# Attention without gate products: transposes in two places, two raw query buffers, the softmax scale on the queries, the maximum written negated

## The reference

```python
def softmax_probs(q, k, scale):
    s = jnp.einsum('bqhd,bkhd->bhqk', q, k).astype(jnp.float32) * scale
    return jax.nn.softmax(s, axis=-1)
# latent attention: 4 heads of 64 + 32, scale (64 + 32) ** -0.5
p = softmax_probs(qb, k, scale).astype(v.dtype)
return jnp.einsum('bhqk,bkhd->bqhd', p, v)
# differential attention: 4 heads with 2 maps of width 32, scale 32 ** -0.5
p = softmax_probs(q1b, k1, scale) - lam * softmax_probs(q2b, k2, scale)
return jnp.einsum('bhqk,bkhd->bqhd', p.astype(v.dtype), v)
```

## Time and profile before

| | |
|---|---|
| median of three runs | 4644.32 us |
| profiled execution | 4637.01 us, its span 4635.2 us |
| PE busy | 3676.0 us (79%) |
| DVE busy | 1965.0 us (42%) |
| ACT busy | 1243.7 us (27%) |
| POOL busy | 1066.2 us (23%) |
| mean granted clock of TensorE | 0.891 |

### The profile page before, as it was taken

One profiled execution on the slowest core, in us unless ns is written; L12 is line 12 of the kernel. 1 busy time (PEld: TensorE's weight loads), 2 busy tenths in 40 slices (PEclk: granted clock), 3 DMA queues, 4 the chain that ended last, 5 costly groups with the idle time before them and its releaser, 6 DMA issues. The chain is left out here.

```text
span 4635.2 us, 63721 instructions
## 1 busy us (share of the span) xinstructions
PE 3676.0 (79%) x25724; PEld 2856.5 (62%) x25724; DVE 1965.0 (42%) x3281; ACT 1243.7 (27%) x2126; POOL 1066.2 (23%) x1114
## 2 busy tenths in 40 slices
PE   5987987466886999897776878987666879998677
PEld 2764656355675777786662665665455757776565
DVE  4224432455345555203553324432554355554255
ACT  2102321344122323213301202321443223232340
POOL 2001001322113343223401101102331034333250
PEclk7978988688898999998987889998788989999898
DMA  4101013100101111335634101014011121111472
GB/s 165 40 34 42 18 34 94 40 26 18 58 29 59 50 44 45 100 118 164 233 105 159 52 32 45 26 33 116 27 31 37 38 65 50 53 53 52 159 252 91
DMA packets 202584, 334.45 MB, mean 72 GB/s; under 512 B 22976, under 2 KB 96448, under 8 KB 200640
## 3 DMA queue, kind: packets, MB, share of 16 engines
q1 hardware_dynamic: 173504, 283.34, 19.3%
q10 hardware_dynamic: 28800, 47.20, 2.8%
HBM read 249.45 MB, written 81.00 MB: 71 GB/s over the span
## 5 line engine op out<-in xcount | busy, mean ns | idle before, releaser
L89 PE MATMUL ps<-hh,wh_ds 128*128 128x512 f32 (+1 forms) x1600 | 689.3, 431 | 79.9 <-POOL wl_ds L202 28.7
L90 PE MATMUL ps<-hl,wh_ds 128*128 128x512 f32 (+1 forms) x1600 | 617.3, 386 | 0.0
L91 PE MATMUL ps<-hh,wl_ds 128*128 128x512 f32 (+1 forms) x1600 | 616.2, 385 | 0.0
L89 PEld LDWEIGHTS ps<-hh,wh_ds 128*128 128x128 f32 x1600 | 322.0, 201 | 161.3 <-issue 54.7
L90 PEld LDWEIGHTS ps<-hl,wh_ds 128*128 128x128 f32 x1600 | 322.3, 201 | 58.5 <-issue 16.7
L91 PEld LDWEIGHTS ps<-hh,wl_ds 128*128 128x128 f32 x1600 | 319.6, 200 | 58.5
L1060 DVE TENSOR_REDUCE mx_d<-ps 128x1 f32<-128x1280 f32 (+1 forms) x144 | 197.2, 1369 | 252.6 <-PE ps L979 252.5
L200 POOL CAST wh_ds<-raw_ds 128x512 fp32r<-128x512 f32 x160 | 107.8, 674 | 792.4 <-DMA raw_ds<-in_d_wmerge 309.2
L933 PE MATMUL ps<-const,qk_da 128*128 128x128 f32 x656 | 131.3, 323 | 163.3 <-ACT pt_da L1101 161.1
L2009 DVE TENSOR_TENSOR T_dr<-T_dr,ps 64x256 f32<-64x256 f32 x400 | 167.6, 419 | 200.3 <-PE ps L1765 191.0
L1131 ACT ACTIVATE qk_da<-ps,nmx_d 128x1280 f32<-128x1280 f32 (+1 forms) x144 | 177.4, 1232 | 229.2 <-DVE nmx_d L1062 229.1
(11 more groups left out here) (322 smaller groups left out, 7977.1 us busy)
## 6 DMA issues: line engine op xcount, KB each, us to landing
gate_sums<-out_ds ACTq DMA_DIRECT2D x160, 256.0 KB, 2.0
raw_ds<-in_d_wmerge SPq DMA_DIRECT2D x128, 256.0 KB, 2.7
logit_mg<-gate_sums SPq DMA_DIRECT2D x128, 256.0 KB, 3.4
w_mod<-in_d_wmod SPq DMA_DIRECT2D x12, 2048.0 KB, 19.7
R_dr<-decay_rows SPq DMA_DIRECT2D x80, 256.0 KB, 4.4
qk_da<-turned_qk SPq DMA_DIRECT2D x32, 320.0 KB, 7.1
q_raw_da<-turned_qk SPq DMA_DIRECT2D x288, 32.0 KB, 1.8
acc_ou<-merged SPq DMA_DIRECT2D x18, 512.0 KB, 5.2
```

The source lines that it names most:

```text
L89: pe.matmul(out, w_hi, x_hi, start=first, stop=False)
L90: pe.matmul(out, w_hi, x_lo, start=False, stop=False)
L91: return pe.matmul(out, w_lo, x_hi, start=False, stop=last)
```

## The change

- The attentions have no gate products: no plan, loads, cuts, moves, `spot` or `settled`. `Dense.ready` gets another lower limit for a stage that plans nothing.
- Groups of transposes are (0,4), (4,2), (6,4) blocks instead of (0,4), (4,4), (8,2). The middle one goes to the upper half of bank 7, where one map's spread inverses also lie; it waits for the move of the group before it there, and in a tile's first head for the last tile's output. The other two share bank 6.
- PE: with two maps each turn group comes after the last piece of scores of a map, the third at the head's end; with one map after the second and the third piece. Value products of a pair come one in head 0 and one in head 2.
- Differential queries have two raw buffers with a semaphore each and two query slots instead of three.
- The scale is multiplied into the queries: on POOL where latent queries are staged, and by two ACT instructions in `prepare_maps`, before the queries are stored.
- `reduce_max(..., negate=True)` writes the negated maximum; L1062 goes. The first map's sum is written where it is kept, so the copy L1049 goes.
- ACT moves the second and third group between the two exponentials; with one map DVE moves groups 0 and 2 ahead of its maximum and inverts there.

```diff
@@ Dense
-        limit = min(self.upto(point), max(self.start, self.end - 2 * KD))
+        low = self.start if self.end > self.start else 0
+        limit = min(self.upto(point), max(low, self.end - 2 * KD))
@@ attention
-    groups = [(at, min(4, key_tiles - at)) for at in range(0, key_tiles, 4)]
+    groups = [(0, 4), (4, 2), (6, 4)] if key_tiles == NT else [(0, CT)]
-    fill.plan((n_tiles - 1) * SPOTS, KD // SPOTS, (7,))
+    SL = 2 // maps
+    value_at = pieces[-1][0] if maps == 2 or len(pieces) == 1 else pieces[-2][0]
-            def turn_bank(count):
-                return m.ps[:, 6, 0:count * P]
+            def turn_bank(g, count):
+                return m.ps[:, 7, BR:BR + count * P] if g == 1 else m.ps[:, 6, 0:count * P]
@@ SP
-                        if g >= 1:
-                            sp.wait_ge(staged, 2 * g)
+                        if g >= 2:
+                            sp.wait_ge(staged, 2 * (g - 1))
-                            sp.dma_start(q_raw[ROPE * a:ROPE * a + ROPE], src).then_inc(q_in, 16)
-                    fill.load(sp, SPOTS * (i - 1))
+                            sp.dma_start(q_raw[ROPE * a:ROPE * a + ROPE, g % 2], src).then_inc(q_in[g % 2], 16)
@@ PE, main loop
+                        pe.wait_ge(staged, maps * (u + 1))
+                        g = 0
                         for a in range(maps):
+                            if u >= SL:
+                                pe.wait_ge(exp_done, (u - SL) * maps + (a + 1))
+                            for at, width in pieces:
+                                mm = pe.matmul(...)
+                                if at + width == keys:
                                     mm.then_inc(scored, 1)
+                                if a == 0 and i and h % 2 == 0 and at == value_at:
+                                    value(i - 1, h // 2)
+                                if before and g < G and (at + width == keys or maps == 1 and at >= value_at):
+                                    turn(*before, g)
+                                    g += 1
+                        while before and g < G:
+                            turn(*before, g)
+                            g += 1
@@ DVE
-                    dve.reduce_max(mx[:, h, a:a + 1], scores(h, a), AX.X).then_inc(dve_step, 1)
-                    dve.wait_ge(dve_step, n + 1)
-                    dve.tensor_scalar(nmx[:, h, a:a + 1], mx[:, h, a:a + 1], -scale, None, ALU.mult).then_inc(maximum, 1)
+                    dve.reduce_max(nmx[:, h, a:a + 1], scores(h, a), AX.X, negate=True).then_inc(maximum, 1)
...
                         if before:
-                            move(*before, on_dve[:1])
+                            move(*before, on_dve)
+                            if maps == 1:
+                                invert(before[1])
@@ ACT
-                        if i and h == LAG:
-                            fill.move(act, SPOTS * i)
...
                             if before and a == 1:
-                                move(*before, on_act[1:2])
+                                move(*before, on_act[1:])
...
-                        if before and maps == 2:
-                            move(*before, on_act[2:])
@@ prepare_maps
-            sp.wait_ge(rotated, 4)
+            sp.wait_ge(q_scaled, 2)
             sp.dma_start(m.d_qk[:, 0:2], raw[0]).then_inc(q_out, 16)
@@ ACT
+            for j in range(2):
+                act.wait_ge(rotated, 2 * (j + 1))
+                act.activation(qk[:, j], qk[:, j], ACT.Copy, scale=ROPE ** -0.5).then_inc(q_scaled, 1)
```

More of the change, by code:

```diff
@@ L834, in attention @@
     on_dve = [g for g in range(G) if g not in on_act]
+    SL = 2 // maps
+    value_at = pieces[-1][0] if maps == 2 or len(pieces) == 1 else pieces[-2][0]
     LAG = 2
     PAIRS = HEADS // 2
-    UNITS = HEADS * maps
-    SPOTS = 4
-    fill = m.dense
-    fill.plan((n_tiles - 1) * SPOTS, KD // SPOTS, (7,))
     with ExitStack() as st:
         sb = lambda n, s, d=F32: st.enter_context(nc.sbuf_tensor(f"{n}_{name}{l}_{t0}", s, d))
-        mx = sb("mx", [P, HEADS, maps])
         nmx = sb("nmx", [P, HEADS, maps])
-        total = sb("total", [P, HEADS, maps])
-        inv = sb("inv", [P, HEADS, maps])
+        mx = sb("mx", [P, HEADS])
+        total = sb("total", [P, HEADS])
+        inv = sb("inv", [P, HEADS])
         own = sb("own", [P, HEADS])
         by = sb("by", [P, 2 * P]) if maps == 1 else None
[L849 to L855, removed]
+        with phase(nc, "q_in0", "q_in1", "q_high", "staged", "scored", "maximum", "exp_done", "inverse", "mixed",
+                   "turned", "moved_a", "moved_d", "valued", "y_done", "mixing", "kept", "spread", "by_ready", "stored") as (
+                block, q_in0, q_in1, q_high, staged, scored, maximum, exp_done, inverse, mixed,
+                turned, moved_a, moved_d, valued, y_done, mixing, kept, spread, by_ready, stored):
+            q_in = [q_in0, q_in1]
             values = m.ps[:, 7, 0:2 * P]
             scales = m.ps[:, 7, 2 * P:4 * P]
+            flat = m.ps[:].rearrange("p b c -> p (b c)")
             def scores(h, a):
@@ L993, in _ @@
-                                if before:
-                                    for g in turns.get(x + a * len(pieces), ()) if G > 1 else ():
-                                        turn(*before, g)
-                            if before and G == 1 and a == maps - 1:
-                                turn(*before, 0)
-                            if h == 1 and i and a == 1:
-                                spot(i - 1, 4)
-                        if h == 2 and i:
-                            value(i - 1, 1)
+                                if a == 0 and i and h % 2 == 0 and at == value_at:
+                                    value(i - 1, h // 2)
@@ L1041, in keep @@
                         dve.wait_ge(spread, i)
-                    dve.tensor_copy(own[:], inv[:, :, 0]).then_inc(kept, 1)
+                    dve.tensor_copy(own[:], inv[:]).then_inc(kept, 1)
                 def mix(i, h):
@@ L1074, in _ @@
                                 mix(*((i, h - 1) if h else (i - 1, HEADS - 1)))
-                        if before:
-                            move(*before, on_dve[1:])
-                            if maps == 1:
-                                invert(before[1])
-                        if maps == 1 and i and h == LAG - 1:
-                            keep(i - 1)
+                                if i and h == LAG:
+                                    finish(i - 1)
                 i = n_tiles - 1
```

109 lines of the change are left out of this document (43 added, 66 removed).

## The result

The kernel after takes 4395.0 us (median of four runs, 4383.5 to 4397.9) beside 4645.5 us for the kernel before on the same chip (4634.9 to 4653.3): a ratio of 0.9458, 95% interval 0.9432 to 0.9483. Forecast were 4455 us, 182 less than the profiled execution of before; measured is 5.4% less. The profiled execution took 4397.9 us, 239 less than the 4637.0 of before.

A forecast was written before the change was run, and what follows sets the result against it. PE bounds latent attention and the last stage; a chain through all engines bounds differential attention. Differential -205, latent -95, context -18, products +154, tails -21, maps +3: -182 from 4637.0 gives 4455 us; own range 4415 to 4500, wider 4395 to 4535.

The forecast's parts named there:

- Products in the last stage: In `apply_gates`, all moved products at 10.9 us per 1000 columns with PE full: 75.4 + 78.2 = +154 us.
- the tails: After PE's last product in `apply_gates`, fewer pieces remain to finish: -11 and -10, together -21 us (bounds 0 and -28).
- Latent attention: Eight-tile latent stages: 27.0 and 27.6 us a tile fall to 21.0 (bounds 18.2 and 25), -95 us together.
- Its stall at the shared bank: Latent attention: bank 6 free after 1.47 us, PE's other work 1.09: 0.38 us stall a head, 1.5 a tile.
- Context tiles of differential attention: Eight 256-key heads: a second raw buffer lets loads run beside POOL and DVE, 5.5 to 3.7 us each, -14 us.
- `prepare_maps`: Two ACT scalings of about 1.3 us each before the query store delay chunk moves: +3 us over both layers.
- 0.36\*2\*3.9 = 2.8. I take 24 us a tile: Differential attention: PE at the lower clock level some 36% of the time adds 2.8 us a tile, giving 24.
- the lower bound of 20.7: Differential attention: DVE's own instructions alone, 20.7 us a tile, the least the tile was expected to take.
- The chain: Differential attention before: no engine full, each head hangs on the last through PE, ACT and DVE, 8 to 9 us a head.
- DVE is next, 20.7 us: Differential attention after the change: DVE's maxima, mixes and output set the pace at 20.7 us a tile, 21.3 with joints.
- The mix at 1.694 us: Differential attention: each of four mixes a tile counted at 1.694 us in DVE's sum.
- faster still: Rival: the engines' own sums hold, 21.3 us a differential and 19.5 a latent tile, giving 4393 us; 10%.

The follow-up runs named there:

- one-buffer run: The kernel after, with one raw query buffer, so SP loads a head's queries only when POOL has finished the head before: 0.9614, 4466 us scaled.
- the run with the maximum twice: The kernel after, with the first map's maximum found twice in differential attention, the extra one to an unread cell: 0.9659, 4487 us scaled.
- the three orders back: The kernel after, with PE's first two turn groups ahead of scores, ACT's last move behind the second exponential, one transpose bank: 1.0050, 4669 us scaled.
- the plain maximum: The kernel after, with the maximum written plain and negated by a second small instruction on DVE: 0.9492, 4410 us scaled.
- the kernel without products: The kernel before, with only the gate products taken out of its attentions, so they fall to the last stage: 1.0074, 4680 us scaled.
- ACT's last move behind: The kernel after, with ACT moving a differential head's last transposed group behind the second exponential instead of ahead of it: 0.9731, 4520 us scaled.

## Why the prediction was wrong, and where it was right

- *Products in the last stage*: +75.4 and +78.2 forecast; +73.4 (215.1 to 288.5) and +79 measured. Right, and so are the tails: 16.7 to 4.5 us and 25.8 to 14.7 up to the next stage's first transfer, -12 and -11 for -11 and -10. PE is full there, so columns times rate is the cost.
- *Latent attention*: 21.0 us a tile forecast and measured, in each tile. Its stall at the shared bank was right in itself: the first and the third group of a head start 1.48 us apart, for 1.47 forecast.

```profile
2827.03 0.60 PE L929 MATMUL ps<-const,e_la 128*128 128x128 f32 x4
...
2828.51 0.63 PE L929 MATMUL ps<-const,e_la 128*128 128x128 f32 x4 [0.22 <-DVE work_la L995]
```

  What the second bank spares, 3.3 us a tile in these orders, the text didn't price. The eight tiles gave 46 in layer 0 for a forecast of 45; in layer 1 some 44 for 49.5. The two context tiles gave 3 for 4.
- *Context tiles of differential attention*: -14 forecast for the second raw buffer, with +3 for `prepare_maps` in two layers. -19 measured for the stretch of layer 0 that holds both, and the one-buffer run gives 17.5 back. Right in kind, some 6 us more than forecast.
- *Differential attention: the step that failed is "0.36\*2\*3.9 = 2.8. I take 24 us a tile".* The tile takes 20.2, below even the lower bound of 20.7. The chain was undone as the text had it (DVE's wait for scores from 83.5 to 2.8 us), and "DVE is next, 20.7 us" was near, but on top I charged PE's clock. Two errors are in it. The clock of 0.82 was carried over from a stage whose gaps the change closes: at 20.2 us PE is busy for 79% instead of 68% and the clock is 1.00. The nine kernels with a lower clock give from 0.97 at 21.6 us to 0.70 at 34.1: on the whole the clock falls as the gaps grow, though not in strict order (0.85 at 29.1 us, 0.81 at 27.2). And where it was low in a DVE-bound tile it was hardly a charge: by the rule of that step a clock of 0.87 beside a DVE head of 6.5 us would add 0.26\*2\*(9.2-6.5) = 1.4 us, in the run with the maximum twice it added at most 0.4 (0.7 in layer 0). Over 15 tile lengths the term is 42 of the 57 us that the tiles were better than forecast.
- *The mix at 1.694 us*: 1.552 measured, 0.6 us a tile, 8 us in all. The mean of the earlier trace rows was one over two groups: of the 64 mixes before, 44 take 1.55 to 1.57 us and 20 take 1.8 to 2.1. In the timeline of the one-buffer kernel a mix that starts beside POOL's subtractions takes 2.09 us, in the kernel after a cast that starts under a mix takes 1.29 instead of 0.40:

```profile
3198.57 0.40 POOL L901 CAST qs_da<-q_raw_da 128x256 fp32r<-128x256 f32 x1 [3.18 <-DMA q_raw_da<-turned_qk]
3199.06 1.53 POOL L904 TENSOR_TENSOR qs_da<-q_raw_da,qs_da 32x256 fp32r<-32x256 f32 x2
...
3199.84 2.09 DVE L1029 SCALAR_TENSOR_TENSOR qk_da<-qk_da,mx_d 128x1280 f32<-128x1280 f32 x1
```

```profile
3143.72 1.55 DVE L1029 SCALAR_TENSOR_TENSOR qk_da<-qk_da,mx_d 128x1280 f32<-128x1280 f32 x1
...
3144.24 1.29 POOL L901 CAST qs_da<-q_raw_da 128x256 fp32r<-128x256 f32 x1 [2.45 <-PE ps L964]
```

  In all thirteen traces each of the 184 mixes longer than 1.6 us ends 1.34 to 1.36 us after the end of a POOL instruction that was under way at its start or began within 0.06 us of it, and the cast above ends 0.26 us after its mix: each waits for the other's instruction to end. In the new order the mix is nearly always first (62 of 64) and POOL, which has time, waits. The Trainium skill's page "SBUF — State Buffer", section Who interferes with whom, says that a DVE instruction with two SBUF inputs, as the mix has, contends with a GpSimd instruction that reads SBUF, and that the order of issue decides who blocks; these rows agree with it. No run changed POOL's work to test it.
- *The rest of the 57 us*, some 7, is rounding up and joints. First tiles gain more than steady ones (67.2 to 41.6 us in layer 0, leave them out), another 6.
- *What the text gave as the mechanism* was right in outline and unequal in its parts: with the products gone, taking the three orders back costs 275 us, one raw buffer 72, the plain maximum 16. These are costs in the finished kernel and overlap: they sum to 363, and the whole step from the kernel without products is 286. With the old orders in place, buffers, maximum and scaled queries together bring 11 us. I named PE's order first; it is the least of the orders. Nor did I see that without products alone the tile would stay at 36 us.
- *Not forecast*: the stages between differential attention and the last stage are 8 us longer in layer 0 and 5 in layer 1. Right behind the attention PE waits 11.4 us for DVE's weights where it waited 8.0. Why is open; it takes 13 us of the gain back.
- *The rivals*: "faster still", 4393 us, had the time to 2 us, with 10%. Its reason, "the engines' own sums hold", is right for differential attention (it had 21.3) and wrong for latent attention (19.5; 21.0 measured): that the two met at the measured time is in part luck.
- *Smaller slips*: 3.9% less holds against the profiled 4637.0 us; against the median it is 4.1%. The chain was put at 8 to 9 us a head, where 37.5/4 is 9.4. A result within 23 us of no change would have needed 159 to 205 us less than counted, not 130 to 180. PE's own work in a differential tile was put at 13.7 us; the profile has it busy for 15.9, which DVE's 19.3 covers.

## What to carry to other kernels

Don't carry a stage's granted clock over a change that closes that stage's gaps, and charge a low clock only where PE is what the stage waits for. Work that fills the gaps of a chain is nearly free: before moving it out, ask whether the chain goes too, since moving the products alone cost 34 us; and ask whether it could stay once the chain is gone, which was not tried here. In a loop over engines look for every instruction that empties a buffer and stands behind a long one (here a move of 0.6 us behind an exponential of 1.33): such orders and a second bank were worth 275 us. What one part costs in the finished kernel is no share of the gain: such costs overlap.

## What the runs showed of the hardware

- The clock in one stage, with PE's busy share (which itself grows when the clock falls), layer 1: 1.00 at 77 to 79%, 0.97 at 77%, 0.94 at 73%, 0.87 at 70%, 0.85 at 68%, 0.81 at 71%, 0.78 at 69%, 0.71 at 62%, 0.70 at 65%. The kernel before had 0.86 at 68%, and the kernel with one raw buffer, whose gaps are long and irregular, 0.89 at 76%. So the share alone doesn't give the clock: at 68 to 71% it lies anywhere from 0.78 to 0.87.
- The same 40 value matmuls took 2.40 us at a granted clock of 1.00 and 4.54 at 0.50 (1.2 GHz, the kernel with ACT's last move behind); with the level changing under them, values between.
- Negating a maximum costs nothing that can be seen (1485 beside 1483 ns for 1280 columns).
- A mix takes 1.55 us, or ends 1.35 us after the POOL instruction that it meets at its start, which makes it up to 2.1; a POOL cast of 0.40 us that starts under a mix ends 0.26 us after it.
- With one raw buffer, 3.3 us pass from POOL's last read of it to its next: four transfers issued some 0.47 us apart, and the last landing.
